# Two low subtractions and two high copies of each layer's first norm move to GpSimd

## The reference, cut to what matters

```python
def rmsnorm(x, g):
    xf = x.astype(jnp.float32)
    y = xf * lax.rsqrt(jnp.mean(xf * xf, axis=-1, keepdims=True) + RMS_EPS)
    return (y * g.astype(jnp.float32)).astype(x.dtype)
...
            h = rmsnorm(x, ev_norm[e])
            r, k, v, q_b, c_kv, q_idx, k_idx, w_idx = jnp.split(h @ ev_w_in[e], split_points, axis=-1)
...
            h = rmsnorm(x, od_norm[o])
            q, k, v = jnp.split((h @ od_w_qkv[o]).reshape(b, t, 3, C_HEADS, HEAD_DIM), 3, axis=2)
```

## Time and profile before

| | us |
|---|---|
| median of three runs | 1770.85 |
| lowest, highest | 1770.39, 1771.46 |
| the profiled execution, its device time | 1772.01 |
| its span in the trace | 1770.3 |

### The profile page before, as it was taken

One profiled execution on the slowest core, in us unless ns is written; L12 is line 12 of the kernel. 1 busy time (PEld: TensorE's weight loads), 2 busy tenths in 40 slices (PEclk: granted clock), 3 DMA queues, 4 the chain that ended last, 5 costly groups with the idle time before them and its releaser, 6 DMA issues. The chain is left out here.

```text
span 1770.3 us, 27643 instructions
## 1 busy us (share of the span) xinstructions
PE 1639.7 (93%) x11068; PEld 875.2 (49%) x11197; DVE 1119.3 (63%) x1884; ACT 468.6 (26%) x785; POOL 165.0 (9%) x190
## 2 busy tenths in 40 slices
PE   7999977889889999989998999999899999999996
PEld 6756666755533333333334887664533333333332
DVE  5557977582437767777777543462446777777776
ACT  5253344363211111111112322462211111111112
POOL 2000734410100000000000031120100000000000
PEclk9999999999999999999999999999999999999999
DMA  6441000026689999999995250208599999999993
GB/s 191 120 125 54 7 3 4 4 96 264 247 343 424 428 426 427 427 425 424 427 424 200 81 190 24 96 1 325 201 368 427 427 426 426 426 426 427 425 422 132
DMA packets 100177, 475.37 MB, mean 269 GB/s; under 512 B 26833, under 2 KB 65745, under 8 KB 74448
## 3 DMA queue, kind: packets, MB, share of 16 engines
q1 hardware_dynamic: 96672, 460.99, 64.6%
q0 software_dynamic: 3376, 12.58, 1.8%
HBM read 454.67 MB, written 18.87 MB: 267 GB/s over the span
## 5 line engine op out<-in xcount | busy, mean ns | idle before, releaser
L716 PE MATMUL ps<-w_unit,xT 128*48 128x512 f32 x1024 | 453.6, 596 | 4.3 <-DVE xT L773 4.3
L717 PE MATMUL ps<-w_unit,xT 128*48 128x512 f32 x1024 | 453.6, 596 | 0.0
L818 DVE SCALAR_TENSOR_TENSOR x<-ps,gate_by_expert,x 128x512 f32<-128x512 f32 x512 | 348.3, 743 | 137.9 <-PE ps L768 137.7
L716 PEld LDWEIGHTS ps<-w_unit,xT 128*48 128x48 f32 x1024 | 126.3, 124 | 311.3 <-issue 305.8
L746 PE MATMUL ps<-w_unit,hidT 128*48 128x512 f32 x1024 | 249.1, 607 | 12.1 <-issue 12.1
L841 ACT ACTIVATE y_high_low<-y_cut 48x512 fp32r<-48x512 f32 x128 | 80.4, 628 | 403.2 <-DVE y_cut L789 400.8
L768 PE MATMUL ps<-y_high_low,slots_to_tokens 128*128 128x512 f32 x512 | 155.5, 425 | 10.8 <-DVE y_high_low L793 8.0
L768 PEld LDWEIGHTS ps<-y_high_low,slots_to_tokens 128*128 128x128 f32 x512 | 86.9, 190 | 126.6 <-issue 61.1
L1291 PE MATMUL ps<-hT_high,w_high 128*128 128x512 f32 (+1 forms) x336 | 137.5, 409 | 9.5 <-DVE hT_low L1186 3.9
L1293 PE MATMUL ps<-hT_high,w_low 128*128 128x512 f32 (+1 forms) x336 | 133.8, 398 | 0.0
L1292 PE MATMUL ps<-hT_low,w_high 128*128 128x512 f32 (+1 forms) x336 | 133.5, 397 | 0.0
(11 more groups left out here) (375 smaller groups left out, 2073.3 us busy)
## 6 DMA issues: line engine op xcount, KB each, us to landing
w_unit<-in_moe_w SPq DMA_DIRECT2D x184, 2048.0 KB, 27.7
w_unit<-in_moe_w SPq DMA_DIRECT2D x16, 1024.0 KB, 32.5
x_rows<-sorted_rows SPq DMA_DIRECT2D x64, 192.0 KB, 26.5
w_unit<-in_od_w_qkv SPq DMA_DIRECT2D x12, 1024.0 KB, 5.8
w_raw<-in_ev_w_in SPq DMA_DIRECT2D x10, 1024.0 KB, 6.0
sorted_rows<-bias SPq DMA_DIRECT2D x32, 192.0 KB, 5.6
w_unit<-in_ev_w_out SPq DMA_DIRECT2D x2, 2048.0 KB, 10.9
w_unit<-in_od_w_out SPq DMA_DIRECT2D x2, 2048.0 KB, 10.3
```

What stands on the lines that cost most here:

```text
L716: nc.tensor.matmul(ps_1[0:MB, :], xT[b][:, k, :], w1[:, k, :], start=k == 0, stop=k == KD - 1)
L717: last = nc.tensor.matmul(ps_3[UP:UP + MB, :], xT[b][:, k, :], w3[:, k, :], start=k == 0, stop=k == KD - 1)
L818: nc.vector.scalar_tensor_tensor(out=xs, in0=ps_c[i % 4][:, :], scalar=gate(t), in1=xs, op0=ALU.mult, op1=ALU.add).then_inc(added, 1)
```

## The change

Of the eight chunks GpSimd now takes low 1 and low 4 (from VectorE) and high 2 and high 5 (from ScalarE), in both layers. It takes them in order of k, each behind mask k. They count on two semaphores of their own, and every wait on the high or low parts becomes a wait for the old and, where one of GpSimd's chunks is among them, the new semaphore. The buffers stay two and two. GpSimd's four instructions stand in its queue ahead of all it did in these stages before: in layer 0 the building of masks and selectors now follows high 5.

```diff
+        self.pool_high_done, self.pool_low_done = c.sem("hT_pool_high_done"), c.sem("hT_pool_low_done")
+
+    POOL_HIGH, POOL_LOW = (2, 5), (1, 4)
+
+    def wait_high(self, eng, k):
+
+        on_pool = sum(1 for i in self.POOL_HIGH if i <= k)
+        eng.wait_ge(self.high_done, k + 1 - on_pool)
+        if on_pool:
+            eng.wait_ge(self.pool_high_done, on_pool)
...
     def ready(self, pe, k):
 
         pe.wait_ge(self.edge, 2)
-        pe.wait_ge(self.high_done, k + 1)
-        pe.wait_ge(self.low_done, k + 1)
+        self.wait_high(pe, k)
+        self.wait_low(pe, k)
...
                         if k >= 2:
-                            act.wait_ge(self.low_done, k - 1)
+                            self.wait_low(act, k - 2)
...
-                    if k >= 1:
+                    if k >= 1 and k - 1 not in self.POOL_HIGH:
                         act.wait_ge(self.masked, k)
...
                     if k >= 2:
-                        dve.wait_ge(self.high_done, k - 1)
-                        dve.wait_ge(self.low_done, k - 1)
+                        self.wait_high(dve, k - 2)
+                        self.wait_low(dve, k - 2)
...
-                    dve.wait_ge(self.masked, k + 1)
-                    nc.vector.tensor_tensor(self.low[:, k, 1:T + 1], self.full[k % 2], self.cut[k % 2],
-                                            ALU.subtract).then_inc(self.low_done, 1)
+                    if k not in self.POOL_LOW:
+                        dve.wait_ge(self.masked, k + 1)
+                        nc.vector.tensor_tensor(self.low[:, k, 1:T + 1], self.full[k % 2], self.cut[k % 2],
+                                                ALU.subtract).then_inc(self.low_done, 1)
+
+            @block.gpsimd
+            def _(pool):
+                for k in sorted(self.POOL_HIGH + self.POOL_LOW):
+                    pool.wait_ge(self.masked, k + 1)
+                    if k in self.POOL_LOW:
+                        nc.gpsimd.tensor_tensor(self.low[:, k, 1:T + 1], self.full[k % 2], self.cut[k % 2],
+                                                ALU.subtract).then_inc(self.pool_low_done, 1)
+                    else:
+                        nc.gpsimd.tensor_copy(self.high[:, k, 1:T + 1],
+                                              self.cut[k % 2]).then_inc(self.pool_high_done, 1)
...
             pool.wait_ge(hT.edge, 2)
-            pool.wait_ge(hT.low_done, KD)
+            hT.wait_low(pool, KD - 1)
```

More of the change, by code:

```diff
@@ L1147, in __init__, with wait_low @@
         self.high_done, self.low_done, self.edge = c.sem("hT_high_done"), c.sem("hT_low_done"), c.sem("hT_edge")
+        self.pool_high_done, self.pool_low_done = c.sem("hT_pool_high_done"), c.sem("hT_pool_low_done")
[5 more added lines that the diff above has]
+            eng.wait_ge(self.pool_high_done, on_pool)
+    def wait_low(self, eng, k):
+        on_pool = sum(1 for i in self.POOL_LOW if i <= k)
+        eng.wait_ge(self.low_done, k + 1 - on_pool)
+        if on_pool:
+            eng.wait_ge(self.pool_low_done, on_pool)
     def ready(self, pe, k):
         pe.wait_ge(self.edge, 2)
-        pe.wait_ge(self.high_done, k + 1)
-        pe.wait_ge(self.low_done, k + 1)
+        self.wait_high(pe, k)
+        self.wait_low(pe, k)
     def evacuate(self, nc, ps):
```

## The result

The changed kernel takes 1775.15 us (median of 19 runs, 1772.69 to 1781.23) against 1770.54 for the kernel before (19 runs, 1768.43 to 1775.42): a ratio of 1.0026, interval 1.0019 to 1.0034. Forecast was 1773.3, in 1771.3 to 1776.3, with most of the chance on a difference within 0.2%. The time lies in the range and the sign of the sum was right, but the cost is 4.6 us and not 2.5, somewhat beyond the 0.2% that I had called the likeliest bound.

What follows compares the result with a forecast made beforehand. TensorE's operand arrival was taken to bound the kernel: 2.0 us in layer 1 plus 0.5 in layer 0 gave 2.5, so 1774.5 profiled; the runs' median lies 1.2 lower, hence 1773.3, eight in ten within 1771.3 to 1776.3.

Steps and rivals of the forecast that it cites:

- What bounds the kernel: Both norms: only TensorE's operand arrival counts; layer 1 pays any chain delay whole, layer 0 has 1.8 us of slack.
- Durations: GpSimd's instructions in both norms: subtraction 1.27 us (bounds 1.04 and 1.45), copy about 0.6 (bounds 0.5 and 1.27).
- Exclusion and walk: Layer 1's norm, chain stepped through with VectorE and GpSimd shutting each other out: chunk 7 starts 2.0 us later.
- rival 2: Both norms: no exclusion between such short instructions, 0.95 late in layer 1, 0.2 in layer 0: +1.2, 1772.0; chance 0.1.
- the lost relief: Layer 1's norm: the 2 x 0.61 and 2 x 0.52 us taken off VectorE and ScalarE turn into waiting.
- Rival 3: The relief counts: with slack in the buffers layer 1 ends 1.0 earlier, layer 0 gains nothing: -1.0, 1769.8; chance 0.06.
- Layer 0: Layer 0's norm: chunk 7 +0.4 us, mask building's collisions 0.1, in all +0.5; building and weight group 1 stay hidden.
- Rival 4: Layer 0: TensorE's clock rises later after the new gap ahead of chunk 1: in all +5.4, 1776.2; chance 0.07.
- rivals 4 and 5: Rival 4, and the fifth: a slow copy, or waits and collisions at their upper bound, +3.5 to +5; chance 0.09.
- its own signs: Wrong if masks keep 0.42 beside GpSimd, the copy takes far over 0.6, or the clock changes anywhere.

Runs made afterwards that it cites:

- the border's dummies: Changed kernel with 32 dummy matmuls added behind the last output of layer 1's projection, before stick-breaking attention: 1774.92 us, 1.0024 against the kernel before.
- the kernel with more dummies: Changed kernel with 16, 12, 8, 16, 12, 8, 6 dummies behind layer 1's chunks 0 to 6: 1773.55 us, 1.0018; again 1774.0 us, 1.0023.

## Why the prediction was right, and where it fell short

**What bounds the kernel.** Right. In layer 1 the chain's delay goes whole into the start of the scores (148.9 to 151.0); in layer 0 most of it disappears behind TensorE's slack.

**Durations.** GpSimd's subtraction was put at 1.27 and took 1.27 to 1.30; the copy at 0.6 plus 0.3 to 0.5 of being shut out, and took 1.13. Being shut out for 0.5 it would be 0.6 alone, though no run shows it alone. The output type costs nothing that shows.

**Exclusion and walk.** Right: masks 2 and 5 near 1.2 and chunk 7 at 9.5 us behind chunk 0 were forecast, 1.16 to 1.18 and 9.49 came. The parts, 1.21 and 0.77, came as the walk gives them, and rival 2 (no exclusion) falls. By the rule of the Trainium skill ("SBUF — State Buffer", Who interferes with whom) the second of two such instructions blocks until the first ends, whatever their shapes; the trace agrees, up to the 0.14 us by which the hold ends before the recorded end.

**The reason given for the lost relief.** Wrong, though its number was right. The prediction said that relief turns into waiting "because with two buffers of each kind chunk k + 2 can't pass chunk k". Four buffers changed nothing. What GpSimd does from SBUF, VectorE can't do its masks and low parts beside, so each moved instruction is inserted in VectorE's own line, buffers or not, less the part by which the hold ends early: a subtraction of 1.27 in place of one of 0.61 (+1.21 for the two), and a copy of about 0.6 that had cost VectorE nothing on ScalarE (+0.77 for the two). Rival 3 (the relief counts) needed more than buffers; whether operands that don't collide would save it, no run here shows.

**Layer 0.** +0.5 forecast; chunk 7 went from 9.03 to 9.60 us behind chunk 0 and weight group 1 from 34.09 to 34.55. The mask building was hidden as said. The clearing of rows was issued at 39.05, 1.46 behind the 37.59 of before, but that is not the building's doing: the memset it waits for had ended at 34.48, and SyncE's queue had been late by as much since its load of weights at 31.33 instead of 29.86, which follows weight group 1's low part (ended at 31.30 instead of 29.83). The rest of the building ended only at 39.63, not near 34. Rival 4, a later rise of the clock there, did not come (0.79 in 23 to 24, 1.00 from 24 on).

**The term that was missing.** The prediction wrote that a fall in layer 1 was unlikely, since with a gap of 1.39 us the clock had stayed at 1.00. That step failed: it looked at the one gap that was there and not at those behind it, which the change widens. They go from 0.61 and 0.16 to 1.05 and 0.60 us, and the clock falls in all six profiles that have instructions on GpSimd in layer 1 and the old dummies (and in the one with the border's dummies). It did not fall in the three profiles with the old dummies and nothing on GpSimd in layer 1. How wide the gaps must be is not shown: with the copies alone the third was 0.29, and it fell too. Nor did the prediction look at what comes 140 us later. The second fall costs 1.6 us, and with it the marks say 2.04 + 0.5 + 1.6 = 4.1, against 4.1 and 4.6 measured. The chances put 0.16 on a cost above 3.5 us, for other causes; the cause that came was not priced. That the time lies in the range is to that extent luck: the upper edge had been set for rivals 4 and 5, neither of which came. By its own signs the prediction was wrong in one point, "if the clock changes anywhere".

**What stays open.** Why the second fall goes with the first. Both kernels idle for about 2 us at that border, and 140 us of dense matmuls lie between. That it came once without the first shows that the first fall isn't needed. That it was gone with dummies at the border suggests that the idle stretch there is needed, but that is one profile. Whether the first fall raises the chance, or whether it is that the border comes 0.8 us or more later against mask 0, these single profiles can't say: 7 of 7 against 1 of 5 by the one reading, 8 of 9 against 0 of 3 by the other. The distance of 146.8 us between the falls stays the same while the work between them varies by 1.3 us. That speaks for something in time that both falls keep to, rather than for one fall causing the other; what the change does at the border would then be to bring its idle stretch later. No run moves the border alone, so this is argued and not shown. Also open is the remainder: layer 1 alone measured +2.7 where its marks say 3.8, the kernel with more dummies +3.2 and +4.1 where they say 2.5 or 4.1, all within intervals of 1.6 to 2.3 us either way.

## What to carry to other kernels

Before giving GpSimd elementwise work from SBUF to relieve VectorE, look for rows where both worked from SBUF at once: if either takes longer by the other's remainder, the two are one engine for this purpose, and the moved work is paid on VectorE's line at GpSimd's price, with more buffers of no use. A copy that ScalarE did for nothing is not free on GpSimd. And when a change widens the small gaps of a TensorE that lives on dummies, price a fall of its clock even if no single gap is longer than those it had. Read the granted clock in the stages behind it too, and in more than one execution: an idle stretch that cost nothing in one profile was followed by a fall in others.

## What the runs showed of the hardware

- VectorE's mask of 128x512 in int32, SBUF to SBUF, is shut out by GpSimd's subtraction and by its copy (0.42 to 1.16 and 0.83), and its two-input subtraction shuts out GpSimd's copy (1.13). All three were forecast; that four buffers of each kind change nothing of it (chunk 7 at 9.48 instead of 9.49) was not.
- The clock fell among the chunks with no idle stretch of TensorE above 1.41 us there: with nothing on GpSimd, taking out the six dummy matmuls (0.51 us for all six) in each of six gaps was enough (0.54 in 979 to 985, against 1.00 in both profiles of the kernel before).
- An idle border of 2 us between two dense stages was followed by a fall of the clock in 8 profiles and by none in 4, at 1.6 us. One kernel, that with more dummies, had it in one profile and not in the other.
- In seven profiles with two falls these begin 146.8 us apart, whatever the length of the work between (149.7 to 151.1 us from mask 0 to the scores).
